# Rows of expert weights gathered into longer runs: an MoE kernel whose loads go from 4 KB to 16 and 8 KB per descriptor

## The chip, the cores and the metric

One Trainium2 chip, one of its NeuronCores. The metric is the device time of one execution in microseconds (us). Times of the kernel before and of the changed kernel are medians of several runs; the profile is one execution of its own, and its times are counted from its first instruction.

## The reference

The reference is a two-layer decoder trunk over 512 tokens of width 1024, float32. Each layer has a mixer (layer 0: retention and pooling; layer 1: sparse latent attention), a normalisation, a mixture of experts, a second normalisation and a gated injection. The change touches only the mixture of experts. There each token picks one of 4 groups and in it 2 of 8 experts, so that 1024 (token, expert) pairs fall on 32 experts. Cut to what matters:

```python
def run(args):
    tok, e = args
    h = xt[tok] @ w_gu[e]              # w_gu[e]: 1024 x 1024 float32, gate and up side by side
    a, b = jnp.split(h, 2, axis=-1)
    return (jax.nn.silu(a) * b) @ w_down[e]    # w_down[e]: 512 x 1024 float32

y = jnp.zeros((N, D)).at[row_tok].add(ys * row_gate[:, None])
```

Both products sum over the rows of a weight matrix. A sum may take its terms in any grouping, as long as row r of the weights meets feature r of the other operand.

## The kernel before

The program is written out engine by engine, with semaphores; there is no scheduler. Per layer the stages around the change are `out_projection` (which also starts the first expert loads), `route` (which writes, per expert, the list of its up to 64 tokens), `experts` and `injection`.

In `experts` (L1020 on) each of the 32 experts is worked once per layer with 64 token slots. The pairs `q` = 0, 1 alternate, with two weight areas: `wide` (4 MiB, gate/up, KD = 8 chunks of 128 rows) and `slim` (2 MiB, down, 4 chunks). One more area (`w3`, `w4`, `XT`) takes expert 31 (`load_last_gu`, `load_last_dn`), which is worked as the 29th; the order is 0 to 27, 31, 28, 29, 30. For one expert:

- GpSimd copies the token list and gathers 128 half rows of x (2 KB each) into `xg[q]` (`gather`, L863). Partition u*64+s holds half u of the row of slot s.
- TensorE turns `xg` in four 128x128 transposes (`turn_gathered`, L875), ScalarE copies them into `xeT` (L907), and TensorE does 2 x 16 matmuls with the gate/up weights (`gate_up`, L889). The first half of them waits for the first half of the load, the second for the second.
- ScalarE applies silu (L911), VectorE multiplies by up into `ga` (L914), TensorE turns `ga` in two transposes (`turn_gated`, L896), VectorE copies (L917), and TensorE does 16 matmuls with the down weights (`down`, L902).
- ScalarE scales the result (L1193), and GpSimd scatters it to `y_rows` (`scatter`, L869).

SyncE refills an area as soon as TensorE is done with it: half of gate/up when the first 16 matmuls are done (`s_gu_half`), the other half (`s_gu`), and down (`s_dn`). Each is one DMA of 2 MiB (`load_gu`, L430, twice; `load_dn`, L434). So up to 12 MiB are on their way while TensorE works. In all these loads partition p takes row k*128 + p of chunk k: each run of neighbouring bytes in memory is one row of 1024 floats, 4 KB, and chunk k of the weights meets columns k*128 to k*128+127 of the other operand.

Before the second round of gathers, GpSimd issues eight scatters of 16-byte entries into `table` (L1118), on the same queue as the gathers. `Further` works experts with over 64 tokens; in the runs shown it has nothing to do (64 executions of L914, two layers of 32 experts).

The change touches `load_gu`, `load_dn`, `load_last_gu`, `load_last_dn`, `turn_gathered`, `turn_gated` and the same loads in `Further.sp`.

Of the kernel before, what the change touches and what calls it, by code (L numbers as in the profile page):

```python
# [22 lines left out]
P = 128  # L23
SEQ = 512
D = 1024
T = SEQ // P
KD = D // P
NB = 512
# [9 lines left out]
NE = NG * EPG  # L38
FF = 512
# [11 lines left out]
def build(nc, A, out):  # L51
    ctx = ExitStack()
    ctx.enter_context(nc.allow_non_contiguous_dma(reason="small vectors to one feature per partition"))
    with ctx:
        def sb(name, shape, dt=F32):
            return ctx.enter_context(nc.sbuf_tensor(name, shape, dt))

        def lasting(name):

            return ctx.enter_context(nc.semaphore(name))  # L60
# [26 lines left out]
        def three(ap, b):  # L87
            return ap.rearrange("p (a b) -> p a b", b=b)
# [8 lines left out]
        ident = sb("ident", [P, P])  # L97
# [12 lines left out]
        PS = ctx.enter_context(nc.psum_tensor("PS", [P, 8, NB], F32))  # L110
# [103 lines left out]
        def rows(w, n):  # L214

            return w.rearrange("(k p) n -> p k n", p=P)
# [196 lines left out]
        XT = sb("XT", [P, KD, SEQ])  # L413
# [5 lines left out]
        pair = [(wide[1], slim[0]), (wide[0], slim[1])]  # L419
        last_in = [lasting(f"last_gu_in{l}") for l in range(2)], [lasting(f"last_dn_in{l}") for l in range(2)]  # L420
        gu_in = [[[lasting(f"gu_in{l}{q}{u}") for u in range(2)] for q in range(2)] for l in range(2)]
        dn_in = [[lasting(f"dn_in{l}{q}") for q in range(2)] for l in range(2)]

        def load_gu(eng, l, q, e, halves=(0, 1)):

            for u in halves:
                ks = slice(u * KD // 2, (u + 1) * KD // 2)
                dst = pair[q][0][:, :].rearrange("p (e k n) -> p e k n", e=1, k=KD)[:, :, ks, :]
                src = A["moe_w_gu"][l][bass.ds(e, 1)].rearrange("e (k p) n -> p e k n", p=P)[:, :, ks, :]
                eng.dma_start(dst, src).then_inc(gu_in[l][q][u], 16)  # L430

        def load_dn(eng, l, q, e):
            src = A["moe_w_down"][l][bass.ds(e, 1)]
            eng.dma_start(pair[q][1][:, :].rearrange("p (e k n) -> p e k n", e=1, k=FF // P),  # L434
                          src.rearrange("e (k p) n -> p e k n", p=P)).then_inc(dn_in[l][q], 16)

        def load_last_gu(eng, l):
            for u, w in enumerate((w3, w4)):
                eng.dma_start(three(w[:, :], D), rows(A["moe_w_gu"][l, NE - 1, u * NB:(u + 1) * NB, :], D))\
                   .then_inc(last_in[0][l], 16)  # L440

        def load_last_dn(eng, l):
            eng.dma_start(three(XT[:, :, :].rearrange("p k s -> p (k s)"), D), rows(A["moe_w_down"][l, NE - 1], D))\
               .then_inc(last_in[1][l], 16)


# [18 lines left out]
        with nc.Block() as block:  # L465
            @block.sync
            def _(sp):
                sp.dma_start(PW, A["pool_w"][0].rearrange("g c d -> c g d")).then_inc(s_pool, 16)
                sp.dma_start(w_out0[0], rows(A["ab_w_out"][0, :, 0:NB], NB)).then_inc(s_wout[0], 16)
                sp.dma_start(w_out0[1], rows(A["ab_w_out"][0, :, NB:D], NB)).then_inc(s_wout[1], 16)  # L470
                load_gu(sp, 0, 0, 0)
                load_dn(sp, 0, 0, 0)
# [373 lines left out]
        xg = [w2[:, 0:512], w2[:, 512:1024]]  # L846
        xeT = [three(w2[:, 1024:1536], SLOTS), three(w2[:, 1536:2048], SLOTS)]
        sa, ga = w2[:, 2048:2304], w2[:, 2304:2560]
# [23 lines left out]

        def turn_gathered(pe, q):
            for c in range(4):
                m = pe.transpose(PS[:, q, c * P:(c + 1) * P], xg[q][:, c * P:(c + 1) * P], ident[:, :])  # L875
            return m

        def chunks(*areas):
# [14 lines left out]

        def turn_gated(pe, q):
            for c in range(2):
                m = pe.transpose(PS[:, 4 + q, c * P:(c + 1) * P], ga[:, c * P:(c + 1) * P], ident[:, :])  # L896
            return m

        def down(pe, q, dn):
# [45 lines left out]
        class Further:  # L945
# [21 lines left out]
            def sp(self, sp, count, before):  # L967
                s = self.s
                gu, dn = pair[0]
                def body(i):  # L970
                    e = sp.value_load(R["expert_i"][:, bass.ds(i, 1)], min_val=0, max_val=NE - 1)
                    row = sp.value_load(R["start_i"][:, bass.ds(i, 1)], min_val=0, max_val=NE * TABLE - SLOTS)
                    for u in range(2):
                        sp.dma_start(meta1[u * SLOTS:(u + 1) * SLOTS, :], table[bass.ds(row, SLOTS), :])\
                          .then_inc(s["meta"], 16)
                    sp.dma_start(gu[:, :].rearrange("p (e k n) -> p e k n", e=1, k=KD),
                                 A["moe_w_gu"][self.l][bass.ds(e, 1)].rearrange("e (k p) n -> p e k n", p=P))\
                      .then_inc(s["gu_in"], 16)
                    sp.dma_start(dn[:, :].rearrange("p (e k n) -> p e k n", e=1, k=FF // P),
                                 A["moe_w_down"][self.l][bass.ds(e, 1)].rearrange("e (k p) n -> p e k n", p=P))\  # L980
                      .then_inc(s["dn_in"], 16)
                self.run(sp, count, body, s["sp"], before)

# [23 lines left out]
            def pe(self, pe, count):  # L1007
                s = self.s
                def body(i):
                    pe.wait_ge(s["gath"], 16 * i + 16)  # L1010
                    turn_gathered(pe, 1).then_inc(s["turn"], 1)
                    pe.wait_ge(s["xe"], i + 1)
                    pe.wait_ge(s["gu_in"], 16 * i + 16)
                    gate_up(pe, 1, gu_of[0], 0)
                    gate_up(pe, 1, gu_of[0], 1).then_inc(s["gu"], 1)
                    pe.wait_ge(s["gated"], i + 1)
                    turn_gated(pe, 1).then_inc(s["gturn"], 1)
                    pe.wait_ge(s["gt"], i + 1)
                    pe.wait_ge(s["dn_in"], 16 * i + 16)
                    down(pe, 1, dn_of[0]).then_inc(s["dn"], 1)  # L1020
                self.run(pe, count, body, s["pe"])
# [13 lines left out]
        def experts(l, then_load):  # L1035
# [28 lines left out]
            with nc.Block() as block:  # L1064
                @block.sync
                def _(sp):
                    sp.wait_ge(s_gath[1], 16)
                    load_last_dn(sp, l)
                    more = further.count(sp)
                    with sp.Fori(1, END) as i:  # L1070
                        for q in range(2):

                            wait_alone(sp, s_gu_half[q], i, sp_tick)
                            load_gu(sp, l, q, 2 * i + q, halves=(0,))
                            wait_alone(sp, s_gu[q], i, sp_tick)
                            load_gu(sp, l, q, 2 * i + q, halves=(1,))
                            wait_alone(sp, s_dn[q], i, sp_tick)
                            load_dn(sp, l, q, 2 * i + q)

                    for a, e, (q, i) in ((0, NE - 4, (0, END - 1)), (1, NE - 3, (1, END - 1)), (0, NE - 2, (1, END))):  # L1080
                        sp.wait_ge(s_gu_half[q], i + 1)
                        load_gu(sp, l, a, e, halves=(0,))
                        sp.wait_ge(s_gu[q], i + 1)
                        load_gu(sp, l, a, e, halves=(1,))
                        sp.wait_ge(s_dn[q], i + 1)
                        load_dn(sp, l, a, e)
# [715 lines left out]
        def before_out(l):  # L1802
            def load_first(sp):
                if l == 1:
                    load_gu(sp, 1, 0, 0)
                    load_dn(sp, 1, 0, 0)
                load_last_gu(sp, l)
            return load_first
# [78 lines left out]
```

## Time and profile before

| | |
|---|---|
| median of 3 runs | 1747.21 us (1746.86 to 1748.9) |
| span of the profiled execution | 1738.4 us |
| median less span | 8.8 us |
| TensorE busy | 1445.6 us (83%) |
| VectorE, ScalarE, GpSimd busy | 407.6, 316.3, 219.6 us |
| mean granted TensorE clock | 0.958 of 2.4 GHz |
| bytes moved by DMA | 482.44 MB in 144344 packets |
| experts of layer 0, first transposes to end | about 252 to 743 us |
| experts of layer 1 | about 1149 to 1644 us |

The profiled execution has no end-to-end time of its own beside its span; the runs' median is 8.8 us above the span, and this part lies before the first and behind the last instruction.

How to read it: a matmul row gives the start, the time that TensorE worked on it, and in brackets how long it had been idle before, with what ended that. "PEld" is the load of the stationary operand. A DMA row names the queue (q1 is that of SyncE's DMAs, q0 that of GpSimd's), the number of packets, the megabytes and the share of the 16 DMA engines' time that the packets took. Packet times may overlap, so a share can be a little over 1.

### The profile page before, as it was taken

The numbers are of one execution on the slowest core, as the hardware profiler recorded it, in microseconds if no ns is written. First come the engines' busy times: TensorE is split into PE (matmuls) and PEld (weight loads), VectorE is DVE, ScalarE is ACT, GpSimd is POOL, SyncE is SP. The second block draws the span as 40 slices with busy tenths as digits, with TensorE's granted clock in tenths as the row PEclk, the third lists the DMA queues.
The fourth block names the chain that finished last, engine by engine and source line by source line (L and its number), as shares of the span: only waits on it lengthen the run. The fifth ranks groups of instructions, "written<-read, shape, count | busy, mean of one in ns | idle before, by whom it ended". The sixth has DMA issues, their size and how long they took to land. (4 is left out here: it accounts for less than half of the span.)

```text
span 1738.4 us, 16759 instructions
## 1 busy us (share of the span) xinstructions
PE 1445.6 (83%) x5992; PEld 651.4 (37%) x5992; DVE 407.6 (23%) x972; ACT 316.3 (18%) x656; POOL 219.6 (13%) x319
## 2 busy tenths in 40 slices
PE   7998968777777778879999999967777787778698
PEld 6885542222222222234444565532222222222243
DVE  3425340000000000043167684330000000000062
ACT  3211011110101000122234672111101010101021
POOL 0000022111111111100001241031111111111000
PEclk8999969999999999989999999969999999999989
DMA  7108169999999999864200005399999999999550
GB/s 270 49 25 327 71 226 316 421 420 420 421 421 421 421 421 420 328 247 152 103 0 1 1 2 207 120 238 402 420 421 421 421 421 420 421 420 410 215 206 37
DMA packets 144344, 482.44 MB, mean 278 GB/s; under 512 B 18912, under 2 KB 20964, under 8 KB 144296
## 3 DMA queue, kind: packets, MB, share of 16 engines
q1 hardware_dynamic: 131336, 463.76, 67.6%
q0 software_dynamic: 10752, 16.85, 2.7%
q10 hardware_dynamic: 2208, 1.20, 0.2%
q8 instruction: 28, 0.46, 0.1%
q14 instruction: 20, 0.16, 0.0%
HBM read 474.91 MB, written 23.63 MB: 287 GB/s over the span
## 5 line engine op out<-in xcount | busy, mean ns | idle before, releaser
L889 PE MATMUL PS<-wide,w 128*64 128x512 f32 x1984 | 453.2, 603 | 96.2 <-ACT w L907 50.2
L902 PE MATMUL PS<-slim,w 128*64 128x512 f32 x992 | 241.6, 631 | 44.5 <-DVE w L917 44.5
L889 PEld LDWEIGHTS PS<-wide,w 128*64 128x64 f32 x1984 | 135.2, 138 | 374.7 <-issue 223.9
L914 DVE TENSOR_TENSOR w<-w,PS 128x256 f32<-128x256 f32 x64 | 27.0, 422 | 885.9 <-ACT w L911 885.9
L902 PEld LDWEIGHTS PS<-slim,w 128*64 128x64 f32 x992 | 79.1, 143 | 167.1 <-issue 109.1
L911 ACT ACTIVATE w<-PS 128x256 f32<-128x256 f32 x64 | 24.5, 383 | 517.2 <-PE PS L889 517.2
L1303 PE MATMUL PS<-wide,XT 128*128 128x512 f32 x256 | 111.5, 593 | 0.0
L1193 ACT ACTIVATE w<-PS,w 128x512 f32<-128x512 f32 x64 | 44.0, 687 | 365.3 <-PE PS L902 365.3
L1110 POOL COPY w<-w 128x1 uint32 (+1 forms) x64 | 11.7, 183 | 711.3 <-ACT w L1193 711.3
L896 PE MATMUL PS<-ident,w 128*128 128x128 f32 x128 | 28.0, 301 | 60.1 <-DVE w L914 47.9
L863 POOL DMA_INDIRECT w<-x_rows,w x64 | 67.6, 1056 | 56.9 <-POOL w L1103 55.6
L869 POOL DMA_INDIRECT y_rows<-w x64 | 65.2, 1019 | 55.2 <-POOL w L1110 55.2
L1303 PEld LDWEIGHTS PS<-wide,XT 128*128 128x128 f32 x256 | 48.1, 190 | 57.3 <-issue 57.3
L637 PE MATMUL PS<-wide,slim 128*128 128x512 f32 x128 | 56.0, 594 | 1.1 <-PEq L1696 1.1
L896 PEld LDWEIGHTS PS<-ident,w 128*128 128x128 f32 x128 | 12.8, 141 | 116.5 <-DVE w L914 116.5
L1705 PE MATMUL PS<-w,wide 128*128 128x128 f32 (+3 forms) x128 | 49.7, 474 | 1.5 <-PEq L1456 0.9
L875 PEld LDWEIGHTS PS<-ident,w 128*128 128x128 f32 x256 | 27.4, 143 | 53.5 <-issue 50.3
L1793 POOL TENSOR_SCALAR w<-w 128x128 f32<-128x128 f32 (+3 forms) x32 | 35.5, 1110 | 93.3 <-DVE w L1737 93.3
L169 ACT ACTIVATE XT<-PS 128x512 f32<-128x512 f32 x40 | 21.7, 595 | 138.0 <-PE PS L162 138.0
L875 PE MATMUL PS<-ident,w 128*128 128x128 f32 x256 | 42.9, 291 | 3.0 <-DMA w<-x_rows,w 3.0
L405 PE MATMUL PS<-x_high,w_high 128*128 128x512 f32 x96 | 38.5, 401 | 7.7 <-DVE w_low L343 7.7
L907 ACT ACTIVATE w<-PS 128x512 f32<-128x512 f32 x64 | 37.7, 589 | 31.5 <-PE PS L875 31.2
(221 smaller groups left out, 1544.8 us busy)
## 6 DMA issues: line engine op xcount, KB each, us to landing
wide<-in_moe_w_gu SPq DMA_DIRECT2D x124, 2048.0 KB, 23.7
slim<-in_moe_w_down SPq DMA_DIRECT2D x62, 2048.0 KB, 24.6
w<-in_moe_w_gu SPq DMA_DIRECT2D x4, 2048.0 KB, 19.4
w<-y_rows SPq DMA_DIRECT2D x16, 512.0 KB, 9.2
wide<-in_ple_w_gate SPq DMA_DIRECT2D x4, 2048.0 KB, 13.8
w<-in_ab_w_in SPq DMA_DIRECT2D x2, 2048.0 KB, 13.9
w_in<-in_ab_w_in SPq DMA_DIRECT2D x2, 2048.0 KB, 7.4
x_rows<-X SPq DMA_DIRECT2D x8, 512.0 KB, 3.0
```

The costliest lines, as they stand in the source:

```text
L405: m = pe.matmul(PS[:, j % 8, :], lhsT, rhs, start=(k == 0 and r == 0), stop=(k == KD - 1 and r == 2))
L637: m = pe.matmul(PS[:, 2 * t + c, :], mixed[:, k, t * P:(t + 1) * P], w_halves[c][:, k, :], start=(k == 0), stop=(k == KD - 1))
L863: pool.indirect_dma_start(out=xg[q], out_offset=None, in_=x_half, in_offset=bass.IndirectOffsetOnAxis(ap=index, axis=0), bounds_check=2 * ...
L869: pool.indirect_dma_start(out=y_rows, out_offset=bass.IndirectOffsetOnAxis(ap=index, axis=0), in_=ys[q], in_offset=None, bounds_check=4 * ...
L875: m = pe.transpose(PS[:, q, c * P:(c + 1) * P], xg[q][:, c * P:(c + 1) * P], ident[:, :])
L889: m = pe.matmul(PS[u * SLOTS:(u + 1) * SLOTS, 2 + q, :], xeT[q][:, k, :], gu[k].rearrange("p (a u c) -> p a u c", a=2, u=2)[:, :, u, :], s ...
L896: m = pe.transpose(PS[:, 4 + q, c * P:(c + 1) * P], ga[:, c * P:(c + 1) * P], ident[:, :])
L902: m = pe.matmul(PS[u * SLOTS:(u + 1) * SLOTS, 6 + q, :], gT[:, k, :], dn[k][:, u * NB:(u + 1) * NB], start=(k == 0), stop=(k == FF // P - 1))
L907: return act.activation(xeT[q].rearrange("p (u c) s -> p c u s", u=2), PS[:, q, :].rearrange("p (c u s) -> p c u s", c=4, u=2), ACT.Copy)
L1193: act.activation(ys[q], PS[:, 6 + q, :], ACT.Copy, scale=R["gate_of"][:, bass.ds(expert(q, i), 1)]).then_inc(s_y[q], 1)
L1303: m = pe.matmul(PS[:, 2 + u % 6, :], XT[:, k, t * P:(t + 1) * P], wg[:, k, c * NB:(c + 1) * NB], start=(k == 0), stop=(k == KD - 1))
L1705: pe.matmul(PS[:, j % 2, 0:width[t]], QH[:, h % 2, h // 2, t * P:(t + 1) * P], KH[:, h // 2, 0:width[t]], start=True, stop=True).then_inc( ...
```

## The change

In all loads of expert weights, partition p now takes neighbouring rows. Half u of gate/up is rows u*512 to u*512+511; partition p takes rows u*512 + 4p to u*512 + 4p + 3, which are 16 KB in one run. Down is two halves of 256 rows; partition p takes two neighbouring rows of each, 8 KB in one run. The bytes in a partition keep their place and amount; which row lies there is another. So chunk c of a half holds rows 4p + c (or 2p + c), and the other operand has to be turned by columns c, c+4, c+8, ... (gathered x, a step of 4 floats, 16 bytes) or c, c+2, ... (gated product, a step of 2 floats, 8 bytes). No instruction is added, removed or moved on any engine; a DMA has the same bytes and the same semaphores.

```diff
         def load_gu(eng, l, q, e, halves=(0, 1)):
             for u in halves:
-                ks = slice(u * KD // 2, (u + 1) * KD // 2)
-                dst = pair[q][0][:, :].rearrange("p (e k n) -> p e k n", e=1, k=KD)[:, :, ks, :]
-                src = A["moe_w_gu"][l][bass.ds(e, 1)].rearrange("e (k p) n -> p e k n", p=P)[:, :, ks, :]
+                dst = pair[q][0][:, :].rearrange("p (e u x) -> p e u x", e=1, u=2)[:, :, u, :]
+                src = A["moe_w_gu"][l][bass.ds(e, 1)].rearrange("e (u p c) n -> p e u (c n)", u=2, p=P)[:, :, u, :]
                 eng.dma_start(dst, src).then_inc(gu_in[l][q][u], 16)
 
         def load_dn(eng, l, q, e):
             src = A["moe_w_down"][l][bass.ds(e, 1)]
-            eng.dma_start(pair[q][1][:, :].rearrange("p (e k n) -> p e k n", e=1, k=FF // P),
-                          src.rearrange("e (k p) n -> p e k n", p=P)).then_inc(dn_in[l][q], 16)
+            eng.dma_start(pair[q][1][:, :].rearrange("p (e u x) -> p e u x", e=1, u=2),
+                          src.rearrange("e (u p c) n -> p e u (c n)", u=2, p=P)).then_inc(dn_in[l][q], 16)
...
         def turn_gathered(pe, q):
             for c in range(4):
-                m = pe.transpose(PS[:, q, c * P:(c + 1) * P], xg[q][:, c * P:(c + 1) * P], ident[:, :])
+                m = pe.transpose(PS[:, q, c * P:(c + 1) * P], xg[q].rearrange("p (f c) -> p c f", c=4)[:, c, :],
+                                 ident[:, :])
...
         def turn_gated(pe, q):
             for c in range(2):
-                m = pe.transpose(PS[:, 4 + q, c * P:(c + 1) * P], ga[:, c * P:(c + 1) * P], ident[:, :])
+                m = pe.transpose(PS[:, 4 + q, c * P:(c + 1) * P], ga.rearrange("p (f c) -> p c f", c=2)[:, c, :],
+                                 ident[:, :])
```

`load_last_gu`, `load_last_dn` and the two loads in `Further.sp` change in the same way.

## Rows read from the trace of the kernel before

**Rows 1.** Page, part 2: 40 slices of 43.5 us, busy tenths and GB/s.
```profile
PE   7998968777777778879999999967777787778698
PEclk8999969999999999989999999969999999999989
DMA  7108169999999999864200005399999999999550
GB/s 270 49 25 327 71 226 316 421 420 420 421 421 421 421 421 420 328 247 152 103 0 1 1 2 207 120 238 402 420 421 421 421 421 420 421 420 410 215 206 37
```

**Rows 2.** Windows, the middle of each layer's experts; the columns are named in the first line.
```profile
core 0: us, PE busy (x) PEld busy (x) DVE busy (x) ACT busy (x) POOL busy (x), PEclk, DMA share, GB/s
...
1174.00:1600.00 426.00, 334.14 (x1470) 111.09 (x1468) 23.70 (x56) 42.52 (x82) 66.21 (x108) 0.98 1.02 419
278.00:706.00 428.00, 335.23 (x1496) 112.84 (x1497) 23.27 (x55) 43.31 (x83) 68.14 (x112) 0.99 1.02 420
```

**Rows 3.** Timeline of TensorE: one expert in the middle of layer 0.
```profile
450.51 0.66 PE L875 MATMUL PS<-ident,w 128*128 128x128 f32 x4
452.03 3.65 PE L889 MATMUL PS<-wide,w 128*64 128x512 f32 x16 [0.86 <-ACT w L907]
456.80 3.65 PE L889 MATMUL PS<-wide,w 128*64 128x512 f32 x16 [1.11 <-DMA wide<-in_moe_w_gu]
461.40 0.44 PE L896 MATMUL PS<-ident,w 128*128 128x128 f32 x2 [0.94 <-DVE w L914]
462.51 3.66 PE L902 MATMUL PS<-slim,w 128*64 128x512 f32 x16 [0.67 <-DVE w L917]
466.09 0.66 PE L875 MATMUL PS<-ident,w 128*128 128x128 f32 x4
```

**Rows 4.** Timeline of TensorE: an expert at the end of layer 0.
```profile
701.37 0.66 PE L875 MATMUL PS<-ident,w 128*128 128x128 f32 x4
702.72 7.09 PE L889 MATMUL PS<-wide,w 128*64 128x512 f32 x32 [0.69 <-ACT w L907]
...
715.28 0.66 PE L875 MATMUL PS<-ident,w 128*128 128x128 f32 x4
```

**Rows 5.** Timeline of TensorE: experts 0, 1, 2, then 26 and 27, layer 0.
```profile
251.58 1.12 PE L875 MATMUL PS<-ident,w 128*128 128x128 f32 x4 [1.84 <-DMA w<-x_rows,w]
...
268.47 0.66 PE L875 MATMUL PS<-ident,w 128*128 128x128 f32 x4
...
282.38 0.65 PE L875 MATMUL PS<-ident,w 128*128 128x128 f32 x4
...
661.61 3.65 PE L889 MATMUL PS<-wide,w 128*64 128x512 f32 x16 [1.18 <-DMA wide<-in_moe_w_gu]
...
673.20 0.66 PE L875 MATMUL PS<-ident,w 128*128 128x128 f32 x4
```

**Rows 6.** Windows: rows of 2 KB (25:29), then of 4 KB.
```profile
25.00:29.00 4.00, 4.00 (x19) 3.33 (x18) 2.70 (x2) 3.54 (x3) 0.00 (x0) 1.00 1.05 410
...
1070.00:1086.00 16.00, 16.00 (x39) 7.05 (x38) 5.61 (x8) 0.29 (x1) 0.00 (x0) 1.00 1.03 422
```

**Rows 7.** DMA packets of the same two windows.
```profile
DMA packets 800, 1.64 MB, mean 410 GB/s; under 512 B 0, under 2 KB 0, under 8 KB 800
...
DMA packets 1709, 6.75 MB, mean 422 GB/s; under 512 B 62, under 2 KB 62, under 8 KB 1709
```

**Rows 8.** DMA, layer 0, 300 to 600 us: issues, KB each, median us to landing.
```profile
wide<-in_moe_w_gu SPq DMA_DIRECT2D x38, 2048.0 KB, 23.7
slim<-in_moe_w_down SPq DMA_DIRECT2D x20, 2048.0 KB, 24.4
w<-x_rows,w POOLq DMA_INDIRECT x20, 5.8
```

**Rows 9.** Timeline, loads of the stationary operand in the four transposes.
```profile
450.51 0.42 PEld L875 LDWEIGHTS PS<-ident,w 128*128 128x128 f32 x4 [0.81 <-issue]
```

**Rows 10.** Line L863, the one gather issued at 263.1 us (expert 2's rows).
```profile
L863 POOL DMA_INDIRECT w<-x_rows,w x1: 1066/1066/1066, 263.1 to 263.1; - x1
...
DMA to landing us min/median/max: 15.1/15.1/15.1
```

**Rows 11.** Window and DMA queues while the table scatters run, 262 to 276 us.
```profile
262.00:276.00 14.00, 11.85 (x58) 3.97 (x56) 0.84 (x2) 1.56 (x3) 3.68 (x6) 1.00 1.08 128
...
q1 hardware_dynamic: 424, 1.68, 97.2%
q0 software_dynamic: 169, 0.09, 9.9%
```

More of the change, by code:

```diff
@@ L433, in load_dn @@
             src = A["moe_w_down"][l][bass.ds(e, 1)]
-            eng.dma_start(pair[q][1][:, :].rearrange("p (e k n) -> p e k n", e=1, k=FF // P),
-                          src.rearrange("e (k p) n -> p e k n", p=P)).then_inc(dn_in[l][q], 16)
+            eng.dma_start(pair[q][1][:, :].rearrange("p (e u x) -> p e u x", e=1, u=2),
+                          src.rearrange("e (u p c) n -> p e u (c n)", u=2, p=P)).then_inc(dn_in[l][q], 16)
         def load_last_gu(eng, l):
             for u, w in enumerate((w3, w4)):
-                eng.dma_start(three(w[:, :], D), rows(A["moe_w_gu"][l, NE - 1, u * NB:(u + 1) * NB, :], D))\
-                   .then_inc(last_in[0][l], 16)
+                eng.dma_start(w[:, :], A["moe_w_gu"][l, NE - 1, u * NB:(u + 1) * NB, :]
+                              .rearrange("(p c) n -> p (c n)", p=P)).then_inc(last_in[0][l], 16)
         def load_last_dn(eng, l):
-            eng.dma_start(three(XT[:, :, :].rearrange("p k s -> p (k s)"), D), rows(A["moe_w_down"][l, NE - 1], D))\
+            eng.dma_start(XT[:, :, :].rearrange("p k s -> p (k s)").rearrange("p (u x) -> p u x", u=2),
+                          A["moe_w_down"][l, NE - 1].rearrange("(u p c) n -> p u (c n)", u=2, p=P))\
                .then_inc(last_in[1][l], 16)
@@ L975, in body @@
                           .then_inc(s["meta"], 16)
-                    sp.dma_start(gu[:, :].rearrange("p (e k n) -> p e k n", e=1, k=KD),
-                                 A["moe_w_gu"][self.l][bass.ds(e, 1)].rearrange("e (k p) n -> p e k n", p=P))\
+                    sp.dma_start(gu[:, :].rearrange("p (e u x) -> p e u x", e=1, u=2),
+                                 A["moe_w_gu"][self.l][bass.ds(e, 1)].rearrange("e (u p c) n -> p e u (c n)", u=2, p=P))\
                       .then_inc(s["gu_in"], 16)
-                    sp.dma_start(dn[:, :].rearrange("p (e k n) -> p e k n", e=1, k=FF // P),
-                                 A["moe_w_down"][self.l][bass.ds(e, 1)].rearrange("e (k p) n -> p e k n", p=P))\
+                    sp.dma_start(dn[:, :].rearrange("p (e u x) -> p e u x", e=1, u=2),
+                                 A["moe_w_down"][self.l][bass.ds(e, 1)].rearrange("e (u p c) n -> p e u (c n)", u=2, p=P))\
                       .then_inc(s["dn_in"], 16)
```

## The prediction, made before the changed kernel was run

> **What bounds the kernel now.** I read the 40 slices first [rows 1]. Two long stretches, one per layer, have the DMA engines at 9 of 10 and 420 or 421 GB/s in every slice while TensorE stands at 7 or 8. The windows over their middle say it closer: 419 and 420 GB/s at a DMA share of 1.02 [rows 2], with TensorE busy for 334 of 426 us. A rate that does not move for 400 us beside an engine with gaps is a full resource. The timeline of one expert shows the gap: TensorE is idle for 1.11 us in the middle of gate/up, and what ends that is the load of `wide` [rows 3]. From one expert's transposes to the next's it takes 466.09 - 450.51 = 15.58 us. At the end of the layer, where the loads are ahead, the same work takes 715.28 - 701.37 = 13.91 us [rows 4]. So in the middle TensorE has 1.67 us of slack per expert, and loads set the pace.
>
> How many experts go by that pace: expert 2 starts at 282.38 and expert 27 at 673.20, the last idle time that names a weight load is at 661.61, in expert 26 [rows 5]. The 25 experts 2 to 26 took 390.8 us, 15.63 each. Their 25 loads are the chain; layer 1 has the same windows [rows 2], so I take it as equal. A load lands 23.7 to 24.4 us after its issue [rows 8], though 2 MiB at 421 GB/s need 5.0: some 20 us of work always wait at the DMA engines. The engines never run dry there, and how fast they go is all that counts.
>
> **The loads.** A load keeps its bytes and gets fewer, longer packets. Two windows with the queue full and a single row size price a packet. With rows of 2 KB: 410 GB/s, 800 packets of 2 KB. With rows of 4 KB: 422 GB/s [rows 6, 7] (62 small packets among 1709 change nothing). Per engine, a sixteenth: 2048 B in 79.9 ns, 4096 B in 155.3 ns. A straight line through both is 75.4 ns per 2 KB and 4.5 ns per packet, whatever its size. As a check: one expert has 6 MiB in 4 KB packets, 96 per engine, and the gather and scatter, of which I take about 4 rows of 2 KB each per engine (64 valid half rows over 16 engines): 96 x 155.3 + 8 x 79.9 = 15.55 us, against 15.58 in the trace.
>
> By this line 16 KB take 8 x 75.4 + 4.5 = 607.7 ns instead of 621.2, and 8 KB 306.1 instead of 310.6. Per expert and engine, gate/up has 16 packets of 16 KB (saves 16 x 13.5 = 216 ns) and down 16 of 8 KB (16 x 4.5 = 72 ns): 0.29 us. 25 loads in two layers: 50 x 0.29 = 14.4 us. The pace of an expert would be 15.3 us, still above 13.91, so that all of it is kept.
>
> The line extends two points that are 3% apart; rounding of the rates by 1 GB/s moves the 4.5 ns to between 3.7 and 5.4, and the gain to 12 to 17 us. The least is nothing, if a long run is cut into 4 KB packets anyway or only rows under 4 KB pay. I take 14.4.
>
> The Trainium skill (DMA: Bandwidth & Descriptors, section Where 436 GB/s comes from) gives 435.2 GB/s as the ceiling of the 16 ports. The line's limit for endless packets is 16 x 2048 / 75.4 = 434.6 GB/s, so the trace agrees with that page, and 16 KB packets would come to within 1% of it.
>
> **The transposes.** Six transposes per expert now load their stationary operand with a step of 16 bytes (four) or 8 bytes (two). No row of before has such a step. Four contiguous loads take 0.42 us, 105 ns each [rows 9]. Least: the same, 0. Twice as long: 6 x 0.105 = 0.63 us per expert. Four times, as if each element cost a fetch of its own: 6 x 0.315 = 1.89 us. Where loads set the pace, slack of 1.67 - 0.29 = 1.38 us covers the first two cases. There is no cover for expert 0 (its first half issues the first refill) and for the five experts behind 26: 6 per layer, 12 in all. So 0, or 12 x 0.63 = 7.6 us, or for four times see below. I take 0, as the nearest row is the plain load, and keep 7.6 in the range.
>
> The Trainium skill (SBUF — State Buffer, section Door 1: The DMA port swizzle) speaks against the change: lines are 16 bytes, and accesses want at least two hits in a line. By this rule the four loads with the 16-byte step have one hit each and the two with 8 bytes are free. If one hit meant twice the time, that would be 4 x 0.105 x 12 = 5.0 us of the gain.
>
> **SyncE and the other queues.** SyncE issues the same DMAs in the same order. GpSimd's gathers share the DMA engines. In the middle a gather lands after 5.8 us [rows 8] and its buffer is read two experts (31 us) after the turn that freed it; even 10 us more stay hidden. The tight one is expert 2's: issued at 263.1 behind eight table scatters, landed 15.1 us later at 278.2 [rows 10], used at 282.38: 4.2 us of margin.
>
> **Sum.** 1747.2 - 14.4 + 0 = 1732.8; in the profile the span goes from 1738.4 to about 1724. I forecast 1733 us.
>
> **Rivals.**
> *A, packets of any size are already at line rate.* For it: 2 KB to 4 KB is worth only 3%, and 420 may be what memory gives. Against: the line fits the pace of an expert within 0.03 us. Time: 1747, or up to 1752 if the transposes cost something. By the Trainium skill (DMA: Bandwidth & Descriptors, section Specifications) line rate needs 512 bytes; taken alone it says this too, but 2 KB and 4 KB rows differ here.
>
> *B, strided weight loads make TensorE the bound.* At four times, an expert takes 13.91 + 1.89 = 15.80 us, above the 15.63 of now: 50 x (15.80 - 15.63) + 12 x 1.89 = 31 us, time 1778. Up to 1.38 us per expert only 12 experts pay, and 14.4 / 12 = 1.2 us per expert, about 200 ns per transpose (three times the plain load), is where the change turns slower. Against: one 4-byte element in 0.82 ns is slow reading already.
>
> *C, GpSimd's packets starve behind long ones.* If engines take turns packet by packet, each of GpSimd's waits 608 instead of 155 ns. The gather of 263.1 would land after up to 4 x 15.1 = 60 us. 4.2 us of that are margin and 22 are covered by the work waiting at the engines; 60 - 15 - 26 = 19 us per layer are lost, 38 in all: 1771. It decides from a landing of some 41 us on; below that it costs nothing. Against: not all of the 15.1 us is waiting for turns.
>
> *D, more gain.* Between 262 and 276 us, with table scatters, the engines are at a share of 1.08 but 128 GB/s: 424 packets take 97.2% of 16 x 14 us [rows 11], 0.51 us each. If the 0.36 us more are paid per packet of a load, fewer packets pay less: 26 per engine become 7 to 13, saving 5 to 7 us per layer on the chain of loads. Time: 1719 to 1723. Against: if the scatters' own number sets it, nothing is saved.
>
> **Chances.** Forecast (14 us, transposes free or up to double): 0.49, its own range 1727 to 1741. D 0.12. A 0.18. B 0.10. C 0.11. Runs of this kernel agree within 0.1%, so no change is told within 0.2%, 1743.7 to 1750.7. Faster: 0.49 + 0.12 = 0.61. Same: 0.15 of A and 0.03 of C (where the loss just meets the gain), 0.18. Slower: B 0.10, 0.08 of C, and 0.03 of A (transposes that cost a little), 0.21. The range leaves out B, the 0.08 of C and a little of D: 1718 to 1752.
>
> **What would show it.** The middle windows' GB/s should go from 420 to about 428 (A: 420), the pace of a middle expert from 15.58 to 15.3, packets from 144344 to about 79,000: 64 x 1536 of 4 KB become 64 x 512 (if they stay, runs are cut). The pace at the end of a layer, 13.91, reads the transposes directly: every 0.1 us more is 1.2 us. The wait for the load at a middle expert must still be there; if it is gone, B holds. The landing of the gather near 263 reads C, and the rate and packets at 262 to 276 read D. I am wrong on the mechanism if the time falls while the middle rate stays at 420, or if the rate rises and TensorE does not come earlier.

## The result and the profile after

| | before | changed |
|---|---|---|
| median of 5 runs | 1747.21 us (1745.89 to 1749.97) | 1732.57 us (1732.26 to 1740.3) |
| span of the profiled execution | 1738.4 us | 1730.5 us |
| packets, bytes | 144344, 482.44 MB | 78808, 482.44 MB |

The ratio is 0.9928, 95% interval 0.9914 to 0.9941; a second measurement, in a later session, gave 0.9915, 0.9900 to 0.9930. By the two intervals together, the change makes the kernel 10 to 17 us faster. The two profiled executions differ by less, 7.9 us. Both numbers are right: single executions scatter over up to 10 us, and the profiled execution of before was a fast one (below).

The page of the changed kernel, the same 40 slices as in [rows 1]:

```profile
PE   7998968877877878869999999968878778788698
...
DMA  7108159999999999854200004389999999999450
GB/s 271 49 25 333 67 195 294 428 429 430 427 429 430 429 428 429 327 222 179 103 0 1 1 1 189 122 243 384 429 429 428 430 429 429 429 429 410 200 207 37
```

The plateaus went from 420 to 429 GB/s. The windows over each layer's experts and the window on the last loads ahead of layer 1 (all 16 KB rows by now), to set against [rows 2] and [rows 6]:

```profile
278.00:706.00 428.00, 342.69 (x1508) 118.25 (x1506) 23.67 (x56) 43.86 (x84) 68.67 (x112) 0.99 1.01 424
1174.00:1600.00 426.00, 343.19 (x1504) 118.79 (x1506) 23.67 (x56) 43.53 (x84) 68.69 (x112) 0.98 1.01 426
...
1070.00:1086.00 16.00, 16.00 (x45) 7.58 (x44) 6.45 (x10) 0.29 (x1) 0.00 (x0) 1.00 1.01 432
```

Gate/up in 16 KB packets alone runs at 432 GB/s where 4 KB packets ran at 422. The first two windows also hold the end of the loads, so they stay under 429. One expert in the middle, to set against [rows 3]:

```profile
451.89 0.75 PE L875 MATMUL PS<-ident,w 128*128 128x128 f32 x4
453.42 3.65 PE L890 MATMUL PS<-wide,w 128*64 128x512 f32 x16 [0.78 <-ACT w L909]
457.94 3.65 PE L890 MATMUL PS<-wide,w 128*64 128x512 f32 x16 [0.87 <-DMA wide<-in_moe_w_gu]
462.54 0.50 PE L897 MATMUL PS<-ident,w 128*128 128x128 f32 x2 [0.94 <-DVE w L916]
463.59 3.65 PE L904 MATMUL PS<-slim,w 128*64 128x512 f32 x16 [0.55 <-DVE w L919]
467.18 0.74 PE L875 MATMUL PS<-ident,w 128*128 128x128 f32 x4
```

The pace is 467.18 - 451.89 = 15.29 us instead of 15.58. The load is still waited for (0.87 us), so loads still set it. The transposes are longer: 0.75 and 0.50 us instead of 0.66 and 0.44. At the end of the layer, where nothing is waited for, an expert takes 714.36 - 700.29 = 14.07 us instead of 13.91 [rows 4]:

```profile
700.29 0.75 PE L875 MATMUL PS<-ident,w 128*128 128x128 f32 x4
701.73 7.09 PE L890 MATMUL PS<-wide,w 128*64 128x512 f32 x32 [0.69 <-ACT w L909]
...
714.36 0.75 PE L875 MATMUL PS<-ident,w 128*128 128x128 f32 x4
```

Two things moved besides. The gather of expert 2 landed after 20.5 us instead of 15.1 [rows 10], and TensorE now waits for it (first row below, the matmuls of the timeline). SyncE's DMA instruction for gate/up took a median of 4528 ns and now 333 ns (`load_gu`'s line, 300 to 600 us; second row).

```profile
285.55 0.75 PE L875 MATMUL PS<-ident,w 128*128 128x128 f32 x4 [0.52 <-DMA w<-x_rows,w]
```
```profile
L429 SPq DMA_DIRECT2D wide<-in_moe_w_gu x39: 332/333/333, 305.1 to 596.3; - x39
```

By parts, from the first transposes of each expert in the two profiles:

| us | layer 0 | layer 1 |
|---|---|---|
| start of expert 0 | +2.0 | -1.7 |
| experts 0 and 1 | 30.80 to 31.97 | 30.75 to 31.44 |
| experts 2 to 26, the chain of loads | 390.82 to 383.41 | 392.63 to 385.07 |
| experts 27, 31, 28, 29 | 55.99 to 59.47 | 57.37 to 57.47 |

The chain gave 7.4 and 7.6 us (6.9 and 7.4 in a second profile of the changed kernel, `after_again`). Of the 3.5 us lost at the end of layer 0, 3.2 are in expert 27, which took 17.26 us. It still waited 0.88 us for its load, and its down stage fell to the low clock (5.35 us instead of 3.65):

```profile
675.02 3.65 PE L890 MATMUL PS<-wide,w 128*64 128x512 f32 x16 [0.88 <-DMA wide<-in_moe_w_gu]
...
680.93 5.35 PE L904 MATMUL PS<-slim,w 128*64 128x512 f32 x16 [0.82 <-DVE w L919]
```

Nothing behind it gives that back. In `after_again` expert 27 did neither, and the same four experts took 56.37 us.

### The profile page after: what moved, and what is told of

Read it like the earlier page. It is cut to its first block and busy times, and to the rows that moved or that the text cites. A ratio compares the mean times of both kernels' runs of the same rounds, so it can differ in the third digit from the quotient of the medians.

```text
span 1730.5 us, 16759 instructions
## 1 busy us (share of the span) xinstructions
PE 1455.4 (84%) x5992; PEld 662.9 (38%) x5992; DVE 407.3 (24%) x972; ACT 317.1 (18%) x656; POOL 219.7 (13%) x319
## 2 busy tenths in 40 slices
DMA packets 78808, 482.44 MB, mean 279 GB/s; under 512 B 18912, under 2 KB 20964, under 8 KB 45992
## 5 line engine op out<-in xcount | busy, mean ns | idle before, releaser
L904 PEld LDWEIGHTS PS<-slim,w 128*64 128x64 f32 x992 | 75.5, 142 | 158.8 <-issue 109.1
L897 PE MATMUL PS<-ident,w 128*128 128x128 f32 x128 | 32.3, 334 | 60.2 <-DVE w L916 54.5
L863 POOL DMA_INDIRECT w<-x_rows,w x64 | 67.6, 1056 | 56.9 <-POOL w L1105 55.6
L897 PEld LDWEIGHTS PS<-ident,w 128*128 128x128 f32 x128 | 20.1, 206 | 116.5 <-DVE w L916 116.5
L875 PEld LDWEIGHTS PS<-ident,w 128*128 128x128 f32 x256 | 36.0, 209 | 54.3 <-issue 49.6
L875 PE MATMUL PS<-ident,w 128*128 128x128 f32 x256 | 48.6, 313 | 3.5 <-DMA w<-x_rows,w 3.5
## 6 DMA issues: line engine op xcount, KB each, us to landing
wide<-in_ple_w_gate SPq DMA_DIRECT2D x4, 2048.0 KB, 13.6
w<-in_ab_w_in SPq DMA_DIRECT2D x2, 2048.0 KB, 13.9
```

The costliest lines, as they stand in the source:

```text
L863: pool.indirect_dma_start(out=xg[q], out_offset=None, in_=x_half, in_offset=bass.IndirectOffsetOnAxis(ap=index, axis=0), bounds_check=2 * ...
L875: m = pe.transpose(PS[:, q, c * P:(c + 1) * P], xg[q].rearrange("p (f c) -> p c f", c=4)[:, c, :], ident[:, :])
L897: m = pe.transpose(PS[:, 4 + q, c * P:(c + 1) * P], ga.rearrange("p (f c) -> p c f", c=2)[:, c, :], ident[:, :])
L904: m = pe.matmul(PS[u * SLOTS:(u + 1) * SLOTS, 6 + q, :], gT[:, k, :], dn[k][:, u * NB:(u + 1) * NB], start=(k == 0), stop=(k == FF // P - 1))
```

## Experiments

All ratios are to the kernel before, run on the same chip in the same session, with 95% intervals.

### What makes the loads faster: packet size or neighbouring rows

`near_4k` and `near_2k` keep the changed kernel's rows and transposes, and lay the two halves of gate/up alternately in the area, so that a run ends after 4 or 2 KB. Expert 31's area stays in 16 KB runs. The matmuls read the weights in the new places and cost the same: an expert without waits takes 14.07 us here as well.

```diff
-                dst = pair[q][0][:, :].rearrange("p (e u x) -> p e u x", e=1, u=2)[:, :, u, :]
-                src = A["moe_w_gu"][l][bass.ds(e, 1)].rearrange("e (u p c) n -> p e u (c n)", u=2, p=P)[:, :, u, :]
+                dst = pair[q][0][:, :].rearrange("p (x u n) -> p x u n", u=2, n=1024)[:, :, u, :]    # near_2k: n=512
+                src = A["moe_w_gu"][l][bass.ds(e, 1)].rearrange("e (u p c) (h n) -> p (e u) (c h) n", u=2, p=P, n=1024)[:, u, :, :]
...
+        gu_of = [[pair[q][0][:, :].rearrange("p (c h u n) -> p u c h n", c=4, u=2, n=1024)[:, u, c, :, :]
```

`runs_8k` takes quarters of 256 rows, two neighbouring rows per partition:

```diff
+                dst = pair[q][0][:, :].rearrange("p (e w x) -> p e w x", e=1, w=4)[:, :, 2 * u:2 * u + 2, :]
+                src = A["moe_w_gu"][l][bass.ds(e, 1)].rearrange("e (w p c) n -> p e w (c n)", w=4, p=P)[:, :, 2 * u:2 * u + 2, :]
...
-xg[q].rearrange("p (f c) -> p c f", c=4)[:, c, :]
+xg[q].rearrange("p (w f c) -> p w c f", w=2, c=2)[:, c // 2, c % 2, :]
```

> Same rows in the same partition as in the changed kernel (4p to 4p+3 of each half) and the same strided transposes, but gate/up goes in packets of 4 KB: the two halves' chunks lie interleaved in the area, so no two rows meet. Down stays at 8 KB, expert 31's area at 16 KB. Theory 1, each packet costs 4.5 ns whatever its size: gate/up has 64 packets per engine and expert again instead of 16, 0.22 us per expert more, so pace of a middle expert 15.5 instead of 15.29, time 1732.6 + 50 x 0.22 = 1743. Rival, reading neighbouring rows of memory one after the other is what helps (fewer jumps of 512 KB), and packet size does nothing: pace 15.3, time 1733.

> As near_4k, with gate/up in packets of 2 KB. Theory 1: 128 packets of 79.9 ns per engine against 16 of 607.7 ns, 0.50 us per expert more: pace 15.8, time 1732.6 + 25 = 1758, middle rate about 415 GB/s. Rival (neighbouring rows help, not packet size): pace 15.3, 1733. A second rival, that only packets over 4 KB are cheaper: same as near_4k.

> Gate/up in runs of 8 KB (two neighbouring rows per partition and quarter), all six transposes with a step of 8 bytes, down as in the changed kernel. Theory 1: 32 packets of 306.1 ns against 16 of 607.7 ns, 0.07 us per expert more than the changed kernel: pace 15.36, time 1732.6 + 3.6 = 1736. If packets over 8 KB are what gains: 1740 or more. Transposes: if the step of 16 bytes costs more than that of 8 bytes, the four take less than 0.75 us here; if any step costs the same, 0.75.

| gate/up packets | down | pace by the line | pace measured | GB/s, 380 to 460 us | ratio |
|---|---|---|---|---|---|
| 2 KB, neighbours | 8 KB | 15.77 | 15.80 | 414 | 1.0107 (1.0090 to 1.0123) |
| 4 KB, neighbours | 8 KB | 15.48 | 15.51 | 422 | 0.9981 (0.9968 to 0.9995) |
| 4 KB, apart (before) | 4 KB | 15.55 | 15.58 | 420 | 1 |
| 8 KB | 8 KB | 15.33 | 15.36 | 427 | 0.9926 (0.9913 to 0.9939) |
| 16 KB (changed) | 8 KB | 15.26 | 15.29 | 429 | 0.9928 (0.9914 to 0.9941) |

The line is the prediction's: 75.4 ns per 2 KB and 4.5 ns per packet. Its five values lie 0.03 us under the measured ones each time, over a range of 0.5 us. Rows with neighbours in 4 KB packets are as fast as rows apart, once the longer packets of down are counted. So packet size is shown as the cause, and reading neighbouring rows as such gives nothing. The windows of 380 to 460 us of near_2k, near_4k and runs_8k:

```profile
380.00:460.00 80.00, 61.61 (x276) 22.17 (x274) 4.23 (x10) 8.32 (x16) 12.29 (x20) 1.00 1.04 414
```
```profile
380.00:460.00 80.00, 62.89 (x280) 21.40 (x282) 4.23 (x10) 7.80 (x15) 12.28 (x20) 1.00 1.02 422
```
```profile
380.00:460.00 80.00, 62.93 (x281) 21.05 (x276) 4.67 (x12) 8.18 (x16) 12.28 (x20) 1.00 1.01 427
```

By the ratios, near_2k lost 31 us to the changed kernel where 25 were expected, near_4k 9 where 10 were. In the profiles the 50 experts of the chain took 25.7 and 8.7 us more than in the changed kernel, so the chain is as the line has it. runs_8k was to be 3.6 us slower and is not; the pace of 15.36 is there, so something else gave it back. Two parts are seen. With 8 KB packets the gather of expert 2 lands after 16.3 us (changed: 20.5) and TensorE does not wait. And the slow stretch at the table scatters (below) costs the two layers 22.9 us of loads, against 26.1 and 23.7 in the two profiles of the changed kernel. The rest is inside the intervals.

### What the strided transposes cost

`runs_16k_plain_turns`, repeated as `plain_turns_again`, has the loads of the changed kernel and `turn_gathered` and `turn_gated` of before. `only_gated_strided` has the plain `turn_gathered` alone. `after_again` is the changed kernel beside them. With plain transposes the weight rows meet the wrong features, so the outputs of those kernels are other numbers; the amount of work is the same.

```diff
-                m = pe.transpose(PS[:, q, c * P:(c + 1) * P], xg[q].rearrange("p (f c) -> p c f", c=4)[:, c, :],
+                m = pe.transpose(PS[:, q, c * P:(c + 1) * P], xg[q][:, c * P:(c + 1) * P],
```

> The changed kernel's loads with the transposes of before (contiguous columns), so weight rows meet the wrong features and the expert outputs are other numbers; same work otherwise. It prices the strided transposes. Theory: an expert that waits for nothing goes back from 14.07 to 13.91 us; 12 experts without cover make 1.9 us, and the short wait for the gather in the third expert stays: time about 1731. Rival, the transposes cost nothing or their cost is hidden everywhere: 1732.6. Rival, they hold up more than they show (clock drops): 1728 or less.

> The changed kernel once more, beside the next two on the same chip, as the reference for the price of the strided transposes. Both theories: 0.993 of before.

> The changed loads with contiguous transposes (expert outputs are other numbers), again. Theory 1, the strided transposes cost their own 0.16 us in the 12 experts without cover and nothing else: 1.9 us less than after_again, ratio between them 0.9989. Theory 2, they cost more (an expert of 14.07 instead of 13.91 us takes longer to catch up after each clock drop, so cover is not full in the middle either): 4 us or more less, 0.9975 or lower, with the experts right behind a cold down stage showing 14.0 against 14.16 us.

> The changed kernel with contiguous transposes of the gathered rows (expert outputs are other numbers) and strided ones of the gated product alone. An expert without waits takes 13.91 + 0.07 = 13.98 us. Theory 1: 12 x 0.07 = 0.8 us over plain_turns_again. Theory 2: between the two others, nearer to plain_turns_again (two of six transposes).

| | expert without waits | ratio |
|---|---|---|
| strided, session 1 / session 2 | 14.07 us | 0.9928 / 0.9915 (0.9900 to 0.9930) |
| only gated strided | 13.98 us | 0.9900 (0.9884 to 0.9915) |
| plain, session 1 / session 2 | 13.91 us | 0.9892 (0.9877 to 0.9906) / 0.9893 (0.9876 to 0.9910) |

Per expert the price is certain: 0.16 us, 0.09 for four transposes and 0.07 for two. Loads of the stationary operand, changed kernel, by line:

```profile
L875 PEld LDWEIGHTS PS<-ident,w 128*128 128x128 f32 x256 | 36.0, 209 | 54.3 <-issue 49.6 <-DMA w<-x_rows,w 4.7
...
L897 PEld LDWEIGHTS PS<-ident,w 128*128 128x128 f32 x128 | 20.1, 206 | 116.5 <-DVE w L916 116.5
```

They take 209 ns (step of 16 bytes) and 206 ns (step of 8 bytes); before, 143 and 141. Four in a row take 0.56 us instead of 0.42, so 35 ns each are on the path. In sum for the kernel, the 12 experts without cover make 1.9 us; the pairs of measurements say 6.3 and 3.8 us, each with some 4 us of uncertainty, and only the second pair was measured side by side. The profiles narrow it down. From expert 0's start to expert 30's, both layers together, the changed kernel took 2.9 us more than the plain one in the second pair (`after_again` 945.96, `plain_turns_again` 943.07), and 5.9 in the first, 3.2 of which are expert 27's above. So some 2.8 us lie in the experts: the 1.9, and about 1 us more in the chain. The rows that speak for that are those behind a drop of the clock, where TensorE has no slack and catches up at 14.16 us per expert strided and 14.01 to 14.09 plain; they come two to six times a layer. What the comparisons have above that is not shown to be the transposes: in the second pair's profiles another 4.1 us lie between the layers' experts, where the code is the same (423.2 against 419.0 us).

The stride can also be put elsewhere. VectorE writes the gated product in the order of the down rows, and ScalarE copies x with permuted columns for `x_rows`:

```diff
-            return dve.tensor_tensor(ga, sa, PS[:, 2 + q, FF // 2:FF], ALU.mult)
+            return dve.tensor_tensor(ga.rearrange("p (c f) -> p f c", c=2), three(sa, 2), three(PS[:, 2 + q, FF // 2:FF], 2), ALU.mult)
...
+                            act.activation(XC[:, t - 1, :].rearrange("p (u c f) -> p u c f", u=2, c=4),
+                                           X[:, t - 1, :].rearrange("p (u f c) -> p u c f", u=2, c=4), ACT.Copy)\
```

> The changed kernel's loads with contiguous transposes: VectorE writes the gated product in the order of the down rows, and ScalarE makes a copy of x with permuted columns, from which x_rows is stored (8 more ScalarE copies, about 1.1 us each, beside other work). Theory from the runs with plain turns: 6 us faster than the changed kernel, ratio to before 0.989 to 0.990; an expert without waits takes 13.91 us. Rival: the 6 us came from where the clock happened to drop, and only 2 us are there: 0.9915. If the strided write costs VectorE time, its multiplication takes over 0.42 us.

It was 0.9958 (0.9942 to 0.9975), 5 us slower than the changed kernel by its first ratio; the expectation was missed. Lines of this kernel, VectorE's product and ScalarE's copy:

```profile
L922 DVE TENSOR_TENSOR w<-w,PS 128x256 f32<-128x256 f32 x64 | 38.3, 598 | 862.0 <-ACT w L919 862.0
...
L677 ACT ACTIVATE w<-X 128x1024 f32<-128x1024 f32 x8 | 16.6, 2077 | 0.0
```

The product takes 598 ns instead of 421, on the path between silu and transposes; an expert without waits takes 14.09 us, no less than the strided transposes' 14.07. A copy takes 2.08 us, not 1.1. The stride was moved to engines where it costs as much on the path. Where the 5 us lie is not shown: in its profile the experts of both layers took 945.5 us, no more than in the changed kernel.

### The table scatters

The window of [rows 11] had shown 128 GB/s from 262 to 276 us. In the changed kernel the same window and its packets are:

```profile
262.00:276.00 14.00, 11.85 (x56) 4.12 (x54) 0.84 (x2) 1.65 (x3) 5.17 (x8) 1.00 1.08 136
```
```profile
q1 hardware_dynamic: 179, 1.89, 107.0%
q0 software_dynamic: 177, 0.01, 0.9%
```

179 packets of weights instead of 424 took as much time, 1.34 us each instead of 0.51, for about the same bytes. The cost of the stretch does not go by the packets of the loads. To price it, the scatters go behind the last gather, where the loads are over (nothing reads the table before):

```diff
-                    for c in range(2 * T):
-                        pool.indirect_dma_start(
...
+                            if (q, i) == (0, PAIRS - 1):
+                                list_entries()
                             put_rows(q, i)
```

> The kernel before, with the eight table scatters of each layer issued at the end of the experts (after the last gather) instead of ahead of expert 2's gather. Theory: from 262 to 276 us the engines move 128 GB/s instead of 421 because of the scatters; that is 14 x (1 - 128/421) = 9.7 us of loads per layer, on the chain of loads: 19 us faster than before (ratio 0.989), expert 2 to 27 in 381 us instead of 390.8. Rival: the slow stretch is covered by the work that waits at the engines and by TensorE's own pace at the start: no change, 0 us.

> The changed kernel with the table scatters late. Theory: both gains add: 0.9928 of before less 19 us, ratio 0.982; the wait for the gather of expert 2 (0.52 us) goes, its landing falls from 20.5 to about 8 us. If long packets had already given back part of the slow stretch (rival D of the prediction), this gains less than before_table_late does: under 14 us over the changed kernel.

> All together: 16 and 8 KB runs, contiguous transposes by permuted copies, table scatters late. Theory: 0.982 less 0.003, ratio 0.979 to before, some 1710 us where before takes 1747.

> Gate/up in runs of 8 KB, table scatters late. Theory (per-packet cost): 0.07 us per expert in the chain more than after_table_late; with about 13 experts per layer still waiting for loads the whole chain still counts, 3.6 us: ratio to before 0.982 to 0.983. Rival: shorter packets let gathers through sooner and it is as fast as after_table_late, 0.980.

| scatters late, with | ratio | median, before in its session |
|---|---|---|
| loads of before | 0.9911 (0.9896 to 0.9925) | 1726.64, 1742.43 us |
| changed loads | 0.9802 (0.9789 to 0.9814) | 1708.06, 1742.43 us |
| changed loads, plain transposes by copies | 0.9825 (0.9808 to 0.9842) | 1710.30, 1742.43 us |
| 8 KB runs | 0.9809 (0.9794 to 0.9823) | 1710.39, 1743.93 us |

The window of after_table_late:

```profile
262.00:276.00 14.00, 11.85 (x56) 4.12 (x54) 0.84 (x2) 1.65 (x3) 2.45 (x4) 1.00 0.99 386
```

386 instead of 136 GB/s. What the stretch costs can be worked out from windows over the 38 us that begin 6 us behind expert 0's start, as 38 x (1 - rate / rate of the plateau). It is 11.0 and 12.4 us in the two layers before, 13.6 and 12.5 in the changed kernel (11.2 and 12.5 in `after_again`) and 12.5 and 10.5 in `near_2k`. So it is the same within 2 or 3 us for packets of 2 to 16 KB. With late scatters it is 1.9 and 0.8, and 1.8 and 0.2. Only the place of the scatters was varied, not their number.

The gather of expert 2 lands after 5.4 us in after_table_late, where some 8 were expected, and is not waited for. Experts 2 to 26 of layer 0 took 380.3 us with the loads of before (390.8) and 370.8 us with the changed ones (383.4): 10.5 and 12.6 us, where 9.7 had been worked out. In time it is worth 15.5 us before, and 22 or 20 us with the changed loads, by the first or second ratio of the changed kernel (it was not run side by side with after_table_late). That is not less than before, where a long packet that already spares part of it would have left under 14.

Not all that the experts gained arrived. In the profile of before_table_late both layers' experts, from expert 0's start to expert 30's, took 23.0 us less than before, and the span is 15.2 us shorter. 5.6 us of the difference lie between layer 0's expert 30 and layer 1's expert 0. There TensorE stands idle for 5.30 us ahead of expert 30's down stage, and the profile names nothing that it waits for:

```profile
735.85 5.05 PE L902 MATMUL PS<-slim,w 128*64 128x512 f32 x16 [5.30 <-issue]
```

after_table_late has no such gap, so it is not shown to belong to the move. after_table_late is the fastest of all: 34 us under the kernel before. The expected 0.982 to 0.983 for 8 KB runs came out at 0.981, again no slower than 16 KB within the intervals. The kernel with all changes together was expected at 0.979 and came out at 0.9825, a miss like that of the permuted copies alone.

## Why the prediction was right, and where it was not

**What bounds.** Right: in every kernel here the pace in the middle is that of the loads, with 15.3 to 15.8 us against 13.9 to 14.1 without waits. With late scatters the loads lose less of their lead at the start, and the first 11 to 14 experts of a layer run at TensorE's pace.

**The loads, -14.4 us.** Right in mechanism and size: 7.4 and 7.6 us in the chain, 15.0 in sum (14.3 in the second profile). The rate of the middle was given as 428 GB/s (429 measured), the pace as 15.3 (15.29), the packets as 79,000 (78,808). The price of a packet, 4.5 ns, holds from 2 to 16 KB. That it came out of two windows was in part luck, and the stated 12 to 17 us was too narrow for what they could say. The 2 KB window lasts 4 us, and the same window, in code that no run changed, reads from 392 to 410 GB/s over the 14 profiles. In that of the changed kernel it is this:

```profile
25.00:29.00 4.00, 4.00 (x19) 3.34 (x18) 2.92 (x2) 3.33 (x3) 0.00 (x0) 1.00 1.04 403
```

With 403 instead of 410 the same sum gives 7.3 ns per packet and a gain of 23 us. The seven profiles in which the window holds no packet under 512 bytes read 406 to 410, five of them 410 as in before; the other seven have 3 to 14 such packets and read 392 to 408.

**The transposes, 0.** Too low. The trace shows 0.16 us per expert, 1.9 us over the 12 experts that I counted as uncovered, and the experts of both layers some 2.8 us; the comparisons say 4 to 6 us with wide intervals. The load of the operand is 1.46 times as long (209 against 143 ns), neither the same nor double. The Trainium skill (SBUF — State Buffer, section Door 1: The DMA port swizzle) asks for at least two hits in a 16-byte line, and says in the same place that a stride of up to 4 fp32 is free, which the prediction left out. By the first the step of 8 bytes would be free and that of 16 bytes would cost; by the second both would be free. The runs show neither: both steps cost the same here, 206 and 209 ns against 141 and 143, and `runs_8k`, with a step of 8 bytes in all six, has 208 and 207.

**Gathers.** The margin of 4.2 us for expert 2 was used up (landing 20.5 us, 5.4 more), and 0.5 us of waiting came of it, which I had not put in the sum. The second profile waits in layer 1 instead: 0.6 us, landing 20.0 us; layer 0 lands at 18.6 and does not wait. It is a mild form of rival C, far from the 41 us where it would decide. In the middle the gathers land after 8.2 us instead of 5.8, hidden as said.

**The sum.** One step was wrong: that the 8.8 us between median and span lie outside the program. The profiled execution of the changed kernel took 1732.38 us with a span of 1730.5, so only 1.9 us lie outside, and it is 1.8 to 1.95 in every other run that has both numbers. The profile of before was thus of an execution of about 1740 us, under all five runs shown. So the forecast of the span, 1724, was 6 us too low, while the forecast of the median, 1733, was right, because it was made as a difference. That it was met within half a microsecond is luck. The measured gain is 12.6 us by the first ratio, 14.8 by the second and 14.6 by the medians. By the traces it should be 14 to 15 us, gained in the chain, less the 2 to 3 us of transposes and waits outside it that the sum put at nothing: 11 to 13.

**Rivals.** A fell (432 GB/s and the five-point table). B fell: the longer transposes never made TensorE the bound of the middle. C came only as 0.5 or 0.6 us. D fell: at the scatters about the same bytes passed with less than half the packets; but the stretch it pointed to was worth as much as the change or more, 15.5 to 22 us.

## What to carry to other kernels

When loads set the pace for hundreds of microseconds, find in the trace two windows with a full queue and one packet size each. A line through them prices another packet size, and the layout with longer runs is worth its difference. The difference of two rates that are 3% apart is fragile, so read the same window in several profiles, and take none that holds a few small packets. Look in the same stretch for windows where the engines are fully busy at a low rate: some small DMA that nothing waits for may sit on the chain, and moving it costs a few lines. Make the sum as a difference, and do not take the gap between a median and one execution's span as a constant.

## What the hardware showed that was not expected

- A load of the stationary operand, 128x128 float32, takes 143 ns contiguous and 209 or 206 ns at steps of 16 or 8 bytes. VectorE's 128x256 product went from 421 to 598 ns when it wrote its output alternately to the two halves of the row, 512 bytes apart, and read its inputs as before; ScalarE's copy of 128x1024 with a step of 16 bytes in its input took 2077 ns.
- Eight scatters of 128 entries of 16 bytes hold down all loads for 14 us and more: 128 GB/s before and 136 changed in the same window, with the engines' share at 1.08 both times. By the windows of 38 us it costs a layer 10 to 14 us of loads, with packets of 2 KB as with 16 KB.
- A DMA instruction of SyncE for 2 MiB of gate/up took 4528 ns with 512 packets while the queues were full, 373 ns with 256 (`runs_8k`) and 333 ns with 128. It cost nothing that the experts' rows show: the waits there name the landing of a load, with the engines at 420 GB/s throughout.
- TensorE's granted clock drops from 2.4 to 1.2 GHz for some 3.4 us in a down stage. This is such a stage in the profile of before, the matmuls and then the window (PEclk is the third number from the end). Ahead of it TensorE had been idle for 1.27 us, where the expert of [rows 3] has 0.67. The windows of 1 us from 666 to 674 show 1.00, 1.00, 0.55, 0.50, 0.50, 0.74, 1.00, 1.00:

```profile
667.92 5.35 PE L902 MATMUL PS<-slim,w 128*64 128x512 f32 x16 [1.27 <-DVE w L917]
```
```profile
668.00:673.00 5.00, 5.00 (x16) 1.66 (x16) 0.00 (x0) 0.00 (x0) 0.00 (x0) 0.66 1.02 421
```

  It costs 1.7 us in the matmuls. It comes 2 to 6 times a layer, but not once in layer 1 of near_2k. In the profiles seen it comes mostly where experts wait for loads: in before_table_late the first ten or so experts behind expert 2 took 14.0 to 14.4 us each and none had it. Inside the chain the next expert makes most of it up; at expert 27 it stays. That may be part of why executions scatter.
